# One more pair by seven products in the last three steps of the matrix for v, with the sums of its operand tiles made ahead

## The reference, cut to what matters

```python
D_MODEL, SEQ, D_INNER = 2048, 256, 4096
def gmlp_mixer(h, w_in, v_gain, w_s, b_s):      # h = rmsnorm(x), (1, 256, 2048)
    z = h @ w_in                                # w_in (2048, 3 * 4096)
    u, v, gate = jnp.split(z, 3, axis=-1)
    u = jax.nn.gelu(u)
    v = rmsnorm(jax.nn.gelu(v), v_gain)
    vc = v.reshape(bsz, seq // 128, 128, 8, 512)
    sv = jnp.einsum('gpq,bnqgc->bnpgc', w_s, vc) + b_s.T[None, None, :, :, None]
    y = u * sv.reshape(bsz, seq, D_INNER)
    return y, gate
```

## Time and profile before

| what | us |
|---|---|
| median of 3 runs | 2147.68 |
| lowest and highest run | 2147.39, 2149.02 |
| profiled execution, span from first to last instruction | 2146.8 |
| the four steps of the matrix for v, in the trace | 1440.53 to 1611.08 |

### The profile page before, as it was taken

The page is one execution under the profiler, slowest core; times in us unless marked ns, Lnnn a source line. Parts: engine busy times, 40 slices in busy tenths (PEclk is TensorE's granted clock), DMA queues, the critical chain, the costliest instruction groups (busy, mean ns, idle before and its releaser), DMA issues.

```text
span 2146.8 us, 30208 instructions
## 1 busy us (share of the span) xinstructions
PE 2135.6 (99%) x10176; PEld 1788.8 (83%) x10176; DVE 1742.5 (81%) x2125; ACT 1261.2 (59%) x1483; POOL 138.1 (6%) x218
## 2 busy tenths in 40 slices
PE   9999999999999999999999999999999999999998
PEld 9988888888888888888888888888888888888886
DVE  6578788666565698999899887787889999999886
ACT  6465455465544665555555555557667666666565
POOL 2022433101000000000000000000000000000000
PEclk9999999999999999999999999999999999999999
DMA  7666555575555566666666666666666666656664
GB/s 254 182 189 211 157 157 150 174 236 174 183 186 181 186 205 199 198 196 198 203 188 196 200 193 199 192 204 187 206 206 187 188 193 194 193 180 208 203 193 152
DMA packets 211513, 412.35 MB, mean 192 GB/s; under 512 B 13176, under 2 KB 13280, under 8 KB 211296
## 3 DMA queue, kind: packets, MB, share of 16 engines
q1 hardware_dynamic: 208608, 402.70, 60.9%
q0 software_dynamic: 1920, 5.31, 0.8%
q10 hardware_dynamic: 896, 3.15, 0.5%
HBM read 409.01 MB, written 3.16 MB: 192 GB/s over the span
## 4 chain that ended last, share of the span: by engine, by line
PE 96%; DVE 2%; DMA 1%; ACT 0%; issue 0%; DVEq 0%; SPq 0%; ACTq 0%
PE gp L1983 49%; PE gp L1915 33%; PE mx L1983 10%; PE mx L2226 1%; PE mx L2110 1%; DVE w_lo L1194 1%; DMA raw<-a_w_out_in 1%; PE mx L2275 1%; DVE t_lo L1426 0%; DVE ff_lo L1193 0%; PE mx L2113 0%; DMA x_tok<-x_in 0%; PE mx L2107 0%; PE mx L2162 0%; PE mx L2206 0%
## 5 line engine op out<-in xcount | busy, mean ns | idle before, releaser
L615 ACT ACTIVATE w_hi<-raw 128x1024 fp32r<-128x1024 f32 x759 | 797.1, 1056 | 681.6 <-PE gp L1915 246.3
L1194 DVE TENSOR_TENSOR w_lo<-raw,w_hi 128x1024 fp32r<-128x1024 f32 x759 | 921.2, 1230 | 233.8 <-ACT w_hi L615 224.1
L1983 PE MATMUL gp<-w_hi,a_hi 128*128 128x512 f32 x1053 | 413.3, 393 | 0.0
L1983 PE MATMUL gp<-w_lo,a_hi 128*128 128x512 f32 x1053 | 410.1, 389 | 0.0
L1983 PE MATMUL gp<-w_hi,a_lo 128*128 128x512 f32 x1053 | 409.8, 389 | 0.0
L1983 PEld LDWEIGHTS gp<-w_hi,a_hi 128*128 128x128 f32 x1053 | 197.7, 188 | 43.0 <-issue 2.9
L1983 PEld LDWEIGHTS gp<-w_lo,a_hi 128*128 128x128 f32 x1053 | 197.6, 188 | 41.4
L1983 PEld LDWEIGHTS gp<-w_hi,a_lo 128*128 128x128 f32 x1053 | 197.8, 188 | 39.8
L1915 PE MATMUL gp<-w_hi,a_hi 128*128 128x512 f32 x576 | 229.9, 399 | 0.0
L1915 PE MATMUL gp<-w_lo,a_hi 128*128 128x512 f32 x576 | 224.6, 390 | 0.0
L1915 PE MATMUL gp<-w_hi,a_lo 128*128 128x512 f32 x576 | 224.3, 389 | 0.0
(11 more groups left out here) (420 smaller groups left out, 3305.3 us busy)
## 6 DMA issues: line engine op xcount, KB each, us to landing
raw<-a_w_in_in SPq DMA_DIRECT2D x192, 512.0 KB, 4.5
raw<-w_ffn_in_in SPq DMA_DIRECT2D x176, 512.0 KB, 4.5
raw<-w_in_in SPq DMA_DIRECT2D x175, 512.0 KB, 3.9
raw<-w_ffn_out_in SPq DMA_DIRECT2D x88, 512.0 KB, 4.6
raw<-a_w_out_in SPq DMA_DIRECT2D x64, 512.0 KB, 4.9
raw<-w_out_in SPq DMA_DIRECT2D x32, 512.0 KB, 4.0
raw<-w_proj_a_in SPq DMA_DIRECT2D x16, 512.0 KB, 4.6
raw<-w_proj_b_in SPq DMA_DIRECT2D x16, 512.0 KB, 4.7
```

Source lines behind the costliest of these rows:

```text
L615: act.activation(w_hi[:, slot], raw[:, slot], ACT.Copy).then_inc(hi_ready, 1)
L1194: dve.tensor_tensor(w_lo[:, slot], raw[:, slot], w_hi[:, slot], ALU.subtract).then_inc(lo_ready, 1)
L1983: ins = pe.matmul(out_, stat[sp_], mov[mp], start=start and p == 0, stop=stop and p == 2, skip_group_check=True)
```

## The change

The first pair of the steps 1 to 3 of V_IN, u = 0, becomes a mixed pair. Its operand sums come from group 0 of the operand, for which they were not made so far; they get tiles of their own, `s0_hi` and `s0_lo`, and group 0 of this operand now signals `op_ready` after `s_lo` in place of after `stat_lo`. Its weight sums are made at j = 12 and 13 of the step before. In these steps PE begins the mixed banks with u = 0, right behind the last pair of the step before, and waits for `bank_free[1]` ahead of the third product of u = 0. Bank (1, 1) gets its first matmul in u = 1. The last step of V_IN is taken out of the loop on ACT and DVE, since it prepares no sums for a step after it.

```diff
+MIXED_WIDE = (0, 2, 4, 6)
+        SUMS0 = (TURN_H3, )
+        def s_of(n):
+            return (s0_hi, s0_lo) if n == 0 else (s_hi[:, n - 1], s_lo[:, n - 1])
+        WIDE = (V_IN,)
...
-            return MIXED
+            return MIXED_WIDE if k in WIDE else MIXED
...
+        def coming(k, i, j):
+            u = (j + RING) // 2
+            if u in mixed(k, i):
+                return mixed(k, i).index(u)
+            if u == S[k].units and k in WIDE and not (isinstance(i, int) and i == S[k].steps - 1):
+                return len(mixed(k, i))
+            return None
@@ DVE @@
             def double_ahead(k, i, j):
-                u, half = (j + RING) // 2, j % 2
-                if u in mixed(k, i) and half == 0:
-                    weight_sums(k, i, mixed(k, i).index(u), j)
+                n = coming(k, i, j)
+                if n is not None and j % 2 == 0:
+                    weight_sums(k, i, n, j)
                 split(j % RING, after(k, i, RING + j + 1), tiles_ahead(k, i, j))
-                if u in mixed(k, i) and half == 1:
-                    dve.wait_ge(t_hi_ready, pairs(k, i, mixed(k, i).index(u) + 1))
+                if n is not None and j % 2 == 1:
+                    dve.wait_ge(t_hi_ready, pairs(k, i, n + 1))
                     dve.tensor_tensor(t_of(k)[2][:], t_of(k)[0][:], t_of(k)[1][:].bitcast(F32), ALU.subtract).then_inc(t_lo_ready, 1)
@@ ACT; stat_lo and mixed_lo on DVE likewise @@
             def stat_hi(n, turn, gain):
-                if n:
-                    act.wait_ge(op_ready, op0[FFN_IN if turn == TURN_H2 else V_IN] + 4 * n)
+                if n or turn in SUMS0:
+                    if n:
+                        act.wait_ge(op_ready, op0[FFN_IN if turn == TURN_H2 else V_IN] + 4 * n)
                     for m in range(UK):
                         ins = act.activation(a_two[:, m], turn_b[:, m], ACT.Copy, scale=col(gain + 4 * n + m))
...
-                if j == 3 and n:
+                if j == 3 and (n or TURN_H3 in SUMS0):
                     mixed_hi(n, TURN_H3)
@@ PE @@
             def mixed_pair(k, i, u, mid):
...
                 three(mx[:, 0], a11, wt(s0, 0), first, last)
-                three(gp[:, 0, 0], a12, wt(s0, 1), False, False).then_inc(unit_used, 1)
+                if u == 0:
+                    pe.wait_ge(bank_free[0], freed(k, i))
+                three(gp[:, 0, 0], a12, wt(s0, 1), u == 0, False).then_inc(unit_used, 1)
...
                 three(mx[:, 1], s1_, wt(s1, 0), first, last)
-                three(gp[:, 1, 0], s4_, wt(s1, 1), False, False).then_inc(unit_used, 1)
+                if u == 0:
+                    pe.wait_ge(bank_free[1], freed(k, i))
+                three(gp[:, 1, 0], s4_, wt(s1, 1), u == 0, False).then_inc(unit_used, 1)
                 pe.wait_ge(t_lo_ready, pairs(k, i, n + 1))
@@ DVE; ACT likewise @@
             double_step(V_IN, 0, nothing, v_first)
-            double_loop(V_IN, 1, S[V_IN].steps, nothing, no_mid)
+            double_loop(V_IN, 1, S[V_IN].steps - 1, nothing, no_mid)
+            double_step(V_IN, S[V_IN].steps - 1, nothing, no_mid)
```

More of the change, by code:

```diff
@@ L202, in build @@
         small = new("small", [64])
+        s0_hi = new("s0_hi", [4, P], F32R)
+        s0_lo = new("s0_lo", [4, P], F32R)
         assert top[0] <= nc.sbuf_usable_end, top[0]
@@ L429, in pairs @@
                 return n + done_pairs[k]
-            return i * len(MIXED) + (n + len(mixed(k, 0)) - len(MIXED) + done_pairs[k])
+            most = len(MIXED_WIDE if k in WIDE else MIXED)
+            return i * most + (n + len(mixed(k, 0)) - most + done_pairs[k])
+        def coming(k, i, j):
[5 more added lines that the diff above has]
+            return None
         def last_unit(k, i):
@@ L973, in mixed_hi @@
             def mixed_hi(n, turn):
-                act.wait_ge(s_summed, n + (3 if turn == TURN_H3 else 0))
-                act.activation(s_hi[:, n - 1], s_sum[:], ACT.Copy).then_inc(s_hi_ready, 1)
+                act.wait_ge(s_summed, sums_of(n, turn))
+                act.activation(s_of(n)[0][:], s_sum[:], ACT.Copy).then_inc(s_hi_ready, 1)
             def residual(k, turn, gain):
@@ L992, in mid @@
                         stat_hi(n, turn, gain)
-                    if j % units == 5 and n >= 1:
+                    if j % units == 5 and (n >= 1 or n == 0 and turn in SUMS0):
                         mixed_hi(n, turn)
@@ L1096, in _ @@
             double_step(V_IN, 0, v_out, v_first)
-            with act.Fori(1, S[V_IN].steps) as i:
+            with act.Fori(1, S[V_IN].steps - 1) as i:
                 own.enter(i - 1, 6)
                 double_step(V_IN, i, v_out, no_mid)
-                own.leave(S[V_IN].steps - 1)
+                own.leave(S[V_IN].steps - 2)
+            double_step(V_IN, S[V_IN].steps - 1, v_out, no_mid)
             act.sem_inc(sums, 1)
@@ L1501, in double_loop @@
                 with dve.Fori(begin, end) as i:
-                    own.enter(i - begin, 2 * len(MIXED) + 3)
+                    own.enter(i - begin, 2 * len(mixed(k, i)) + 3)
                     double_step(k, i, head, mid)
@@ L1681, in mixed_lo @@
             def mixed_lo(n, turn):
-                dve.wait_ge(s_hi_ready, n + (3 if turn == TURN_H3 else 0))
-                dve.tensor_tensor(s_lo[:, n - 1], s_sum[:], s_hi[:, n - 1].bitcast(F32), ALU.subtract).then_inc(op_ready, 4)
+                dve.wait_ge(s_hi_ready, sums_of(n, turn))
+                hi, lo = s_of(n)
+                dve.tensor_tensor(lo[:], s_sum[:], hi[:].bitcast(F32), ALU.subtract).then_inc(op_ready, 4)
             def residual(k, turn, gain):
@@ L1701, in mid @@
                         stat_lo(n, turn, gain)
-                    if j % units == 6 and n >= 1:
+                    if j % units == 6 and (n >= 1 or n == 0 and turn in SUMS0):
                         mixed_lo(n, turn)
@@ L1993, in operand, with starts @@
                 return [x_[:, UK * u + kk, m * P:(m + 1) * P] for x_ in (a_hi, a_lo)]
+            def starts(k, i, u, half, m):
+                return u == 0 or u == 1 and 0 in mixed(k, i) and (half, m) == (1, 1)
             def plain_pair(k, i, u, mid):
@@ L2005, in plain_pair @@
                             ins = three(gp[:, half, m], operand(k, i, u, kk, m), [w_[:, slot, kk] for w_ in (w_hi, w_lo)],
-                                        u == 0 and kk == 0, u == end and kk == UK - 1)
+                                        kk == 0 and starts(k, i, u, half, m), u == end and kk == UK - 1)
                         if u == end and m == 0:
@@ L2048, in mixed_pair @@
                 else:
-                    s1_, s2_, s3_, s4_ = [[x_[:, MIXED.index(u), q] for x_ in ((sx_hi, sx_lo) if k == AV else (s_hi, s_lo))]
-                                      for q in range(4)]
+                    s1_, s2_, s3_, s4_ = [[x_[:, q] for x_ in ((sx_hi[:, n], sx_lo[:, n]) if k == AV else s_of(u // 2))]
+                                          for q in range(4)]
                 wt = lambda slot, kk: [w_[:, slot, kk] for w_ in (w_hi, w_lo)]
```

13 lines of the change are left out of this document (7 added, 6 removed).

## The result

The changed kernel takes 2162.86 us (median of four runs, 2161.63 to 2164.06); the kernel before, run beside it, takes 2147.71 us (four runs, 2147.39 to 2149.02). The ratio is 1.007, with a 95% interval of 1.0056 to 1.0084: 15.2 us slower. The forecast was 2160.5 us, in a range from 2153 to 2166. The profiled execution took 2161.63 us with a span of 2159.6 us.

What follows compares the result with a forecast made beforehand. PE was taken as the bound, with no margin against DVE's freeing of half 1's banks at the seams. Terms 4.2 + 4.1 + 3.9 + 0.7 = 12.9 us gave 2160.5 us, range 2153 to 2166.

Steps and rivals of the forecast that it cites:

- The bound and the missing margin: Seams between steps: PE is the bound without margin, starting 0.13 us behind DVE's `whole` that frees half 1's banks.
- The ceiling of 2.04 us: Three steps save 0.68 us each, 2.04 us in all, lost because saved matmuls lie ahead of the half 1 wait.
- 4.34 us ahead of `whole`: Each seam: DVE does sums (2.66 us) and `t_lo` (1.68 us) ahead of half 1's `whole`, in a 13.2 us block.
- The seams, 4.2, 4.1 and 3.9: New delays in us of half 1's `whole` at seams 0 to 1, 1 to 2 and 2 to 3.
- What the last sums wait for: Seam 1 to 2: sums of j = 12 wait for the second load, landing 4.95 us after the `w_lo` letting it go.
- Group 0, 0.7 us: FFN_OUT: group 0's operand sums make the next turn wait for `s_lo`, 0.7 us once, between nothing and 1.5 us.
- ACT, nothing: ACT's queue at j = 13: `t_hi` and an earlier wait for the sums fit its idle time and cost nothing.
- Rival (a): DVE's idle time in each step takes the added work: 2147.7 us, or 2145.6 at best; chance 0.08.
- Rival (b): Sums of j = 12 hide ahead of `parts`, only `t_lo` delays `whole`: 5.7 us, 2153.4 us; chance 0.10.
- Rival (c): PE's clock falls behind the three holes at the seams: 5.5 us more, 2166 us; chance 0.10.
- From span to time: Whole kernel: the median lies 0.9 us above the span, turning a forecast span of 2159.7 into 2160.5 us.
- The lengths of the steps: Matrix for v: steps 1 and 2 last about 45.5 us in place of 41.6, and step 3 likewise.

Runs made afterwards that it cites:

- a1_both: Kernel before plus both pieces of the seams' added DVE work (weight sums and `t_lo`), results unused, every product kept: 2162.44 us, ratio 1.0067.
- b1_fill: Changed kernel plus twelve unread matmuls in the hole ahead of the wait for half 1's banks: 2160.46 us, ratio 1.0059 to the kernel before.
- b0_again: The changed kernel run once more, nothing altered: 2162.49 us, ratio 1.0071 to the kernel before.
- b2_order: Changed kernel with DVE's `whole` for half 1 called ahead of `t_lo` and the second `w_lo` at the seams: 2156.99 us, ratio 1.0041 to the kernel before.
- a4_group0: Kernel before plus only the operand sums of group 0, made and not used: 2148.19 us, ratio 1.0001.
- c1_elsewhere: Kernel before plus 1.8 us of dead DVE work at j = 3 of steps 1 to 3 of the matrix for v: 2150.44 us, ratio 1.0012.
- a2_sums: Kernel before plus only the wait for both loads and the four weight sums at j = 12, every product kept: 2157.30 us, ratio 1.0044.
- c2_pool: Changed kernel with the seams' sums and `t_lo` moved to GpSimd and `whole` for half 1 called early: 2161.22 us, ratio 1.0058 to the kernel before.

## Why the prediction was right, point by point

**The bound and the missing margin**. Right, and shown: work on DVE alone (`a1_both`) costs as much as the change, and PE waits for the line named.

**The ceiling of 2.04 us, lost ahead of the wait.** The hole is where this step put it, nine matmuls into each step, and the wait for it is 3.04 us at all three seams. That the saving is worth nothing was not tried apart. `a1_both` keeps the nine matmuls and costs 14.3 us where the change costs 14.5 and 15.2, which fits, but 2.04 us is less than these numbers can tell.

**4.34 us ahead of `whole`.** Right: the block of 13.2 us measured 13.18 us at the first two seams, and the two parts cost 2.6 to 2.9 and 1.7 to 1.9 us a seam when added alone.

**The seams, 4.2, 4.1 and 3.9.** The sum of 12.2 us stood against 13.6 in the profile of the changed kernel. This was right by luck, by two errors of opposite sign, which `b1_fill` separates. With the clock held its seams are 4.0, 2.7 and 3.8 us, 10.5 in all: the term for the seam from step 1 to step 2 was 1.4 us too large. Its premise was that the body of step 1 moves by 3.1 us; in `b1_fill` the sums of the pair ahead start at 1516.05, which is 3.7 us later than in the earlier trace rows, and 2.0 of those it had before the first seam already. So the body moved by 1.7 us. The clock then puts 3.1 us on top in these two profiles (13.6 less 10.5), and 2.0 by the medians of `b0_again` and `b1_fill`.

**What the last sums wait for.** By the forecast it is the landing of the second load. In the changed kernel DVE comes to them from `w_lo`, which waited for ACT, and ACT at 1525.53 and 1526.89 had waited for PE. The landing as the forecast works it out (1520.22 + 2.52 + 4.95 = 1527.69) would fall on the same moment, 1527.77, so this trace can't tell which of the two would have ended last by itself. Two others point to the landing as the last one: DVE is idle ahead of these sums for 0.67 us at the third seam of `b1_fill` (up to 1571.50; the load by the same sum at 1564.14 + 2.52 + 4.95 = 1571.61) and for 0.91 us at the second seam of `b2_order` (up to 1526.69).

**Group 0, 0.7 us.** Its turn starts at 1341.87 in place of 1341.04, and the turn ahead at 1329.41 in place of 1329.24: 0.66 us, with a wait of 0.52 us for `s_lo`. By itself it is below what the runs can tell (`a4_group0`, +0.1 us).

**ACT, nothing.** No wait of PE names `t_hi`; held.

**Rival (a), the idle time takes it.** Refuted for this place: the block at the seam runs for 13.18 us without a pause, and `a1_both` pays for its added work in full. That the shares fit (40.98 against 40.90 us) was sound arithmetic and no argument, since a share can't tell which idle stretch takes work: where `c1_elsewhere` put 1.8 us a step, the idle time took about half, and three steps cost 2.6 us.

**Rival (b), only half of it lies in the way.** Refuted by `a2_sums`: the sums alone cost 9.2 us, more than `t_lo`.

**Rival (c), the clock falls.** Its mechanism is at work, at a smaller price. The windows of the changed kernel behind its three holes:

```profile
1493.86:1499.92 6.06, 6.06 (x15) 4.76 (x15) 5.45 (x7) 5.30 (x9) 0.00 (x0) 0.51 0.60 172
1541.00:1544.16 3.16, 3.16 (x8) 2.48 (x8) 3.09 (x5) 2.75 (x6) 0.00 (x0) 0.50 0.83 201
1586.85:1592.00 5.15, 5.15 (x23) 4.27 (x24) 4.29 (x6) 4.52 (x8) 0.00 (x0) 1.00 0.66 202
```

Behind two of the holes PE ran at 0.51 and 0.50 of its clock (1.2 GHz in place of 2.4) for 15 and 8 matmuls, behind the third one at 1.00. On PE that is 6.06 - 15 x 0.227 = 2.7 us and 3.16 - 8 x 0.227 = 1.3 us. The seams show 3.1 of these 4.0 us (13.6 less the 10.5 of `b1_fill`): the 2.7 us of step 1 stand whole in the second seam (5.4 against 2.7), the 1.3 us of step 2 hardly in the third (4.2 against 3.8). The medians of other executions show 2.0 (`b0_again` less `b1_fill`), and the granted clock says that not every one has the same lower stretches. The rival had 5.5 us, by three stretches of 1.84. I gave it a chance of 0.10 because no row of the kernel before had such a hole; yet the forecast itself made three of 3.0 to 3.5 us. It should have been a term of the sum, not a rival. By the Trainium skill, page "TensorE: Matmul & The Clock Gate", section "Why this matters for your kernels", idle gaps of this kind between bursts are to be avoided for just this reason; the trace agrees behind two of three holes, and `c2_pool` shows the fall behind shorter waits as well (last section).

**The end of the sum.** Seams of 13.6 and group 0 of 0.66 make 14.3 us; the span grew by 12.8 (2146.8 to 2159.6). At the third seam PE was 14.64 us later than in the kernel before, so 1.8 us came back behind it: 0.9 of them are two waits for `sf_lo` in a later product, which the kernel before has and this execution has not; the rest is not assigned. In `b1_fill` the 10.5 + 0.66 = 11.2 us agree with the span (2158.0, 11.2 above 2146.8), but by chance: it was 2.0 us late in step 0, of which group 0 is 0.66, and 1.3 us came back behind the third seam.

**From span to time.** The term of 0.9 us was wrong. A time stands 2.0 us above its span in the changed kernel and 1.7 us in the later runs of the kernel before (2147.53 with 2145.8), so the profiled execution of the kernel before was itself some 0.8 us slower than the median. With it the measured difference is 12.8 + 0.3 (2.0 less 1.7) + 0.8 + 1.2 (the median over the profiled 2161.63) = 15.1 of the 15.2 us. The forecast had 12.9, with the clock left out of the sum.

**The lengths of the steps.** About 45.5 us was said of all three; 48.23, 45.84 and 44.48 were measured. The slower matmuls make step 1 longer, by the 2.7 us that it lies above 45.5.

**Open.** Why the third hole, as long as the others, left the clock alone; why the 1.3 us of slower matmuls in step 2 show as only 0.4 at the next seam (that seam is set by DVE, which may not be late by all of it, but no run isolates this); why the seams of `b1_fill` cost 3.3 us less than its two parts tried apart, and whether the saved matmuls have a share in it; why the start of the matrix for v moves by 0 to 2.4 us. A pair by seven products at another place of the step was not tried. No version here beats the kernel before, and the ceiling of 2.04 us lies below what can be told.

## What to carry to other kernels

Before work is put on a second engine because it has idle time, ask what each idle stretch waits for. Where it waits for a load that the same engine let go, it is slack only for work put behind that instruction and ahead of the wait. What is left over moves the next loads and their idle stretches along: here about half of the added work reached the time. Count what a saving on the bound engine stands ahead of: three matmuls saved ahead of a wait that already ends last need not show in the time, and each us put ahead of what ends that wait cost about one here. When a forecast makes a hole of 2 to 3 us in TensorE's stream, put a possible slower clock behind it into the sum; matmuls that nothing reads, put into the hole, kept it away here without a cost of their own that shows.

## What the runs showed of the hardware

- Holes of 3.42 to 3.44 us from start to start brought the lower clock behind two of three of them in each of two executions (the changed kernel behind the first and the second, `b0_again` behind the first and the third). Shorter holes did it too, at times. In `c2_pool` the clock was 0.52 behind a wait of 2.21 us (1491.33 to 1493.09) and 0.51 behind one of 1.88 us (1583.50 to 1586.60), while it stayed at 1.00 behind waits of 2.13 us in `a2_sums` and 2.15 us in `b2_order`: the length of one hole alone doesn't tell. In `a1_both` two holes a few us apart did it at the first seam (waits of 1.68 and 2.26 us; the clock is 0.64 in the first window below, and 1.00 for the 12 matmuls between the holes in the second) and at the second seam (0.46 and 2.34 us), but not at the third (0.46 and 2.34 us again):

```profile
1494.42:1499.00 4.58, 4.58 (x13) 3.69 (x14) 3.69 (x6) 3.75 (x8) 0.00 (x0) 0.64 0.76 225
1489.16:1492.00 2.84, 2.84 (x12) 2.17 (x12) 2.81 (x3) 2.75 (x7) 0.00 (x0) 1.00 0.24 27
```

- Matmuls that nobody needs made the kernel faster: 36 of them, 2.0 us by the medians of five runs each.
- Beside GpSimd's subtraction, DVE's addition with both inputs in SBUF (`c_part<-c_part`) took 1.81 us and the one with an input in PSUM (`c_part<-mx,c_part`) still 0.69, in `c2_pool` above. By the Trainium skill, page "SBUF — State Buffer", section "SBUF: two separate sides", the two engines share a pair of ports that one of them holds for a whole instruction, and a DVE instruction with two inputs in SBUF needs it against a GpSimd instruction that reads SBUF. The trace agrees: the addition of 0.69 us starts at 1484.02 inside GpSimd's 1483.36 to 1484.65 and isn't held up, the one of 1.81 us starts at 1484.75 with GpSimd's instruction of 1484.73 to 1486.01 and ends 0.55 us behind it.
